# Moving the activation sums of a seven-product matrix scheme from VectorE to GpSimd, with later tile sums and reordered tile loads

## The chip, the cores and the metric

The kernel runs on one core of a Trainium2 chip. The metric is the device time of one execution in microseconds (us). Five engines work side by side: TensorE (PE in the rows; its weight loads are PEld), VectorE (DVE), ScalarE (ACT), GpSimd (POOL) and SyncE (SP, whose queue starts the weight DMAs). Each runs its own list of instructions in order; they meet at semaphores.

## The reference

Two transformer blocks over 256 tokens of width 2048 in float32. What the change touches is the feed-forward part of each block (called MLP here), once per block:

```
hf = rms_norm(x, g_ffn[layer])
x = x + (jax.nn.silu(hf @ w_gate[layer]) * (hf @ w_up[layer])) @ w_down[layer]
```

The hidden width is 5632, so each of the two MLPs streams about 138 MB of weights. The attention parts before and between them are computed by the same kernel and are not changed.

## The kernel before

Every float32 product is made of three passes of TensorE over rounded operands (fp32r): high weight with high activation, high weight with low activation, low weight with high activation. The weights come from memory as a stream of 512 KB units of 128x1024. For each unit ScalarE makes the high half (`split` in its list, L1140, `w_hi<-raw`), VectorE the low half (`split` in its list, L1649, `w_lo<-raw,w_hi`), and TensorE runs 12 matmuls (L622). All three buffers (`raw`, `w_hi`, `w_lo`) have four slots. So ScalarE may be four units ahead of TensorE at most; a unit's DMA starts when VectorE has read the unit four places before it; and the order of everything else is written out by hand as "after so many splits do this" (`steps(n, {k: [...]})`), a table for ScalarE and a like one for VectorE. An engine that waits inside such an entry also holds back its next splits.

An MLP has 3 groups of 3, 4 and 4 pairs of blocks (gate and up), each group followed by two pairs of "down" blocks. A block is 512 output columns for all 256 tokens. For 12 pairs in each MLP, `SEVEN`, the first two weight tiles of both blocks aren't multiplied in the plain way but by seven products of sums (a Strassen-like scheme). That needs:

- **tile sums** on GpSimd (`seven_sums(j)`, L554 to L557, four subtractions of 128x512 for each of two steps), over tiles that GpSimd loads itself (`load_seven(j)`, L538 two transfers of 768 KB, L540 one of 512 KB, into `heads` and, for odd j, `tab`). In the first line of `seven_sums` it waits for the third transfer. ScalarE (L1236, L1240) and VectorE (L1867) then round them (`preparing`, entries at three splits of the pair before).
- **activation sums** on VectorE (`sums_raw`, L1881 over 128x1024 into `tmp_c`, L1882 to L1885 over 128x256 each), then ScalarE's high half of them (`sums_hi`, L1246) and VectorE's low half (`sums_lo`, L1891). They are made three times in an MLP: once from the normed input (in the second pair of the first group, (0, up, 1), after split 7) and twice from the hidden values (in the pairs (0, up, 2) and (1, up, 2), after split 9). ScalarE's entry is at split 7 in the first case and 10 in the two others, VectorE's low half at 9 and at 11.
- **opening** (`open_seven`, L769): 24 matmuls of TensorE over the rounded sums; it waits for `act_ready` (from `sums_lo`) and `seven_ready`, and sits near the end of the pair before. For the first of an MLP it comes after the twelfth unit of (0, up, 1).
- **combining** (`combine`, L1898 to L1902 on VectorE, `first_out` and `third_in` on ScalarE, L1251 and L1256), then **closing** (`close_seven`, L769 again), for which TensorE waits for `combined` and `third_copied`. Where the pair being opened is (1, up, 3), `combine` is VectorE's entry at split 11 of (1, up, 2), right behind `sums_lo(True)`.

GpSimd's list in an MLP is a loop over j: wait until the tiles of j - 1 were used (`products_done`), `load_seven(j)`, `seven_sums(j)`. For the first j of an MLP the load waits for TensorE's second unit of the MLP, and the sums follow at once. During the first 16 units VectorE also transposes and norms the last parts of the activations (L1784, L1753), which TensorE needs from about the thirteenth unit on.

ScalarE's `gated` (L1294) is the gate function (silu) of a finished block, 128x512 twice; in (0, up, 1) it stands behind `sums_hi(False)` in the same entry.

Of the kernel before, what the change touches and what calls it, by code (L numbers as in the profile page):

```python
# [22 lines left out]
F32 = mybir.dt.float32  # L23
F32R = mybir.dt.float32r
I32 = mybir.dt.int32
ALU = mybir.AluOpType
# [8 lines left out]
CB = 4  # L35
NB = CB * P
# [160 lines left out]
def two_blocks(nc: bass.Bass, stream, seven_in, mem_in, mem_tok, x_in, x_tok, p_in, decay_in, vectors, rows_in,  # L197
               head_rows, consts, tables, positions, out):
    with ExitStack() as ctx:
# [3 lines left out]
        def sem(name):  # L203
            return ctx.enter_context(nc.semaphore(name))
# [101 lines left out]
        seven_hi_ready = sem("seven_hi_ready")  # L306
        seven_ready = sem("seven_ready")
        act_summed = sem("act_summed")
        act_hi_ready = sem("act_hi_ready")
        act_ready = sem("act_ready")  # L310
        products_done = sem("products_done")
# [84 lines left out]
        def raw7(step, i, n=1):  # L396
            return tiles(heads, step, i, n)
# [10 lines left out]
        def last_raw(j):  # L408
            return tab[:, 0:STEPS * NB].rearrange("p (s n) -> p s n", s=STEPS) if j % 2 else both_steps(heads, T4)
# [98 lines left out]
        def _(pool):  # L508
# [27 lines left out]
            def load_seven(j):  # L536
                for step in range(STEPS):
                    pool.dma_start(raw7(step, W11, 3), seven_in[j][:, step * 4 * NB:(step * 4 + 3) * NB])\  # L538
                        .then_inc(seven_landed[step], 16)
                pool.dma_start(last_raw(j), seven_in[j].rearrange("p (s n) -> p s n", s=STEPS)[:, :, 3 * NB:])\  # L540
                    .then_inc(last_landed, 16)

            def after_own(ins, n):

                ins.then_inc(pool_done, 1)
                pool.wait_ge(pool_done, n)

            def seven_sums(j):

                pool.wait_ge(last_landed, 16 * (j + 1))  # L550
                for step in range(STEPS):
                    own = 3 * (STEPS * j + step)
                    pool.wait_ge(seven_landed[step], 16 * (j + 1))
                    after_own(pool.tensor_tensor(raw7(step, T3), raw7(step, T2), raw7(step, T1), ALU.subtract), own + 1)  # L554
                    after_own(pool.tensor_tensor(raw7(step, T1), raw7(step, T1), raw7(step, W11), ALU.subtract), own + 2)
                    after_own(pool.tensor_tensor(raw7(step, T2), raw7(step, T2), raw7(step, T1), ALU.subtract), own + 3)
                    pool.tensor_tensor(last_raw(j)[:, step], last_raw(j)[:, step], raw7(step, T2), ALU.subtract)\  # L557
                        .then_inc(seven_summed, 1)

            for j in range(N_SEVEN):  # L560
                if j:
                    pool.wait_ge(products_done, j)
                else:
                    pool.wait_ge(w_used, U_MLP_AT[0] + 2)
                load_seven(j)
                seven_sums(j)

            pool.wait_ge(seven_used, N_SEVEN)
            pool.dma_start(tab[:, :], tables).then_inc(tab_landed, 16)
# [7 lines left out]
            for j in range(N_SEVEN, 2 * N_SEVEN):  # L577
                if j > N_SEVEN:
                    pool.wait_ge(products_done, j)
                else:  # L580
                    pool.wait_ge(w_used, U_MLP_AT[1] + 2)
                load_seven(j)
                seven_sums(j)
            pool.wait_ge(seven_used, 2 * N_SEVEN)
            pool.dma_start(tab[:, 0:2 * T], p_in).then_inc(p_landed, 16)
            load_row(B_ROW, ROWS.index("b_ple_gate_2"), bias_landed)
# [528 lines left out]
        def _(act):  # L1115
# [142 lines left out]
            def mlp(name, next_name, at, which, final=False, beside=None):  # L1258
# [43 lines left out]
                for g, n in enumerate(GROUPS):  # L1302
                    nd = n * CB // UK
                    for p in range(n):
                        pair = g, "up", p
                        j, after = (seventh(which, q) for q in all_pairs[all_pairs.index(pair):][:2])
                        early = {4: [lambda: hidden_hi(p - 1)]} if p else {}
                        if (g, p) == (0, 0):
                            during(2 * NU - 3, at)
                            wait_rows()  # L1310
                            gated()
                            split(3)
                            taken.add()
# [12 lines left out]
                        taken.add()  # L1326
# [300 lines left out]
        def _(dve):  # L1627
# [241 lines left out]
            def sums_raw(hidden, used):  # L1869

                if used:
                    dve.wait_ge(seven_used, used)
                dve.wait_ge(raw_read, units.value())
                if joined[0]:
                    dve.wait_ge(third_copied, joined[0])
                src_hi, src_lo = (mix_hi, mix_lo) if hidden else (norm_hi, norm_lo)
                by_sum = chunks(heads, sums_at(hidden) + CB).rearrange("p (s i n) -> p s i n", s=STEPS, i=4)
                s1, s2, s3, s4 = (by_sum[:, :, i] for i in range(4))
                by_part = tmp_c[:, :].rearrange("p (s i n) -> p s i n", s=STEPS, i=4)
                a11, a21, a12, a22 = (by_part[:, :, i] for i in range(4))  # L1880
# [24 lines left out]
            def mlp(name, next_name, at, which, final=False, beside=None, beside_last=None):  # L1905
# [52 lines left out]
                for g, n in enumerate(GROUPS):  # L1958
                    nd = n * CB // UK
                    for p in range(n):  # L1960
# [749 lines left out]
```

## Time and profile before

| | us |
|---|---|
| median of 3 runs | 2377.13 (2376.47 to 2378.82) |
| the profiled execution | 2374.19 |
| its span in the profile | 2372.0 |
| TensorE idle in the span | 18.5 |
| VectorE, ScalarE, GpSimd busy | 1949.5, 1223.2, 395.5 |

The profile is of one execution. What bounds the kernel is read first from the busy shares; as TensorE is nearly always busy, the few places where it is not are what a change off TensorE can win or lose. They are found with the waits of TensorE and with its busy time in stretches of 10 us; then the timeline around each shows who was late.

### The profile page before, as it was taken

Reading aid. Unit: us, or ns where it says so; the run is one execution under the profiler, and the core shown is the slowest. Engines: PE = TensorE matmul, PEld = TensorE weight load, DVE = VectorE, ACT = ScalarE, POOL = GpSimd, SP = SyncE. Lnnn points to the kernel's source line nnn. Section 1 sums busy time; section 2 is a strip of 40 time slices with the busy share of each in tenths; the row PEclk is TensorE's granted clock in tenths of the full one; section 3 lists DMA queues with packets and bytes.
Section 4 is the critical chain, followed back from the end, with each engine's and each line's share of the span. In section 5 each row is a group of like instructions: output and inputs, shape, how many; then the busy total and the mean of one; then the engine's idle time right before and its main releaser. Section 6 shows DMA issues by size and latency. Waiting matters only on the chain.

```text
span 2372.0 us, 30916 instructions
## 1 busy us (share of the span) xinstructions
PE 2353.5 (99%) x10692; PEld 1957.6 (83%) x10692; DVE 1949.5 (82%) x2542; ACT 1223.2 (52%) x1639; POOL 395.5 (17%) x290
## 2 busy tenths in 40 slices
PE   9999999999999999999999999999999999999999
PEld 8988888878888888888888888877878888888887
DVE  7788887879788977878897977987978898787885
ACT  6554555545455544545554445454545454464563
POOL 1000000211433434200000000021144343520000
PEclk9999999999999999999999999999999999999999
DMA  8755454665757676655555554565565666665655
GB/s 305 238 173 186 159 170 163 208 207 188 246 202 244 207 237 212 224 203 202 185 189 194 192 189 160 195 226 201 187 234 200 246 211 230 226 213 200 211 189 168
DMA packets 130337, 487.43 MB, mean 205 GB/s; under 512 B 14480, under 2 KB 15120, under 8 KB 129568
## 3 DMA queue, kind: packets, MB, share of 16 engines
q1 hardware_dynamic: 116736, 421.32, 53.0%
q0 software_dynamic: 13184, 64.02, 7.6%
q8 instruction: 86, 1.41, 0.2%
q14 instruction: 43, 0.35, 0.0%
q10 hardware_dynamic: 288, 0.33, 0.0%
HBM read 483.51 MB, written 2.10 MB: 205 GB/s over the span
## 4 chain that ended last, share of the span: by engine, by line
PE 93%; DVE 3%; DMA 1%; ACT 1%; POOL 1%; issue 1%; SPq 0%; ACTq 0%; DVEq 0%
PE acc L622 61%; PE pt L622 9%; PE po L622 9%; PE acc L769 4%; PE pt L769 3%; PE po L769 3%; DVE w_lo L1649 1%; DMA tab<-seven_in 1%; PE acc L985 1%; PE acc L627 1%; PE po L968 1%; PE acc L899 1%; DVE tmp_c L1784 1%; DVE norm_lo L1753 1%; PE po L960 1%
## 5 line engine op out<-in xcount | busy, mean ns | idle before, releaser
L1649 DVE TENSOR_TENSOR w_lo<-raw,w_hi 128x1024 fp32r<-128x1024 f32 x796 | 1022.0, 1299 | 314.2 <-ACT w_hi L1140 307.7
L1140 ACT ACTIVATE w_hi<-raw 128x1024 fp32r<-128x1024 f32 x795 | 831.8, 1058 | 784.1 <-PE acc L622 470.6
L622 PE MATMUL acc<-w_hi,norm_hi 128*128 128x512 f32 (+1 forms) x1460 | 568.6, 390 | 1.4 <-DVE norm_lo L1753 1.3
L622 PE MATMUL acc<-w_hi,norm_lo 128*128 128x512 f32 (+1 forms) x1460 | 565.3, 387 | 0.0
L622 PE MATMUL acc<-w_lo,norm_hi 128*128 128x512 f32 (+1 forms) x1460 | 387.8, 388 | 4.1 <-DVE w_lo L1649 4.0
L622 PE MATMUL acc<-w_hi,mix_hi 128*128 128x512 f32 x832 | 325.2, 391 | 0.3 <-ACT w_hi L1447 0.3
L622 PE MATMUL acc<-w_hi,mix_lo 128*128 128x512 f32 x832 | 324.1, 390 | 0.0
L622 PEld LDWEIGHTS acc<-w_lo,norm_hi 128*128 128x128 f32 x1460 | 272.7, 188 | 61.1 <-DVE w_lo L1649 5.4
L622 PEld LDWEIGHTS acc<-w_hi,norm_hi 128*128 128x128 f32 x1460 | 274.1, 188 | 57.6 <-issue 2.5
L622 PEld LDWEIGHTS acc<-w_hi,norm_lo 128*128 128x128 f32 x1460 | 274.1, 188 | 55.1
L622 PE MATMUL acc<-w_lo,mix_hi 128*128 128x512 f32 x832 | 222.5, 389 | 0.0
L622 PEld LDWEIGHTS acc<-w_hi,mix_hi 128*128 128x128 f32 x832 | 156.4, 188 | 33.3 <-ACT w_hi L1447 0.9
L622 PEld LDWEIGHTS acc<-w_lo,mix_hi 128*128 128x128 f32 x832 | 156.1, 188 | 32.8 <-DVE w_lo L1649 0.4
L622 PEld LDWEIGHTS acc<-w_hi,mix_lo 128*128 128x128 f32 x832 | 156.5, 188 | 32.2
L538 POOL DMA_DIRECT2D heads<-seven_in x48 | 26.3, 550 | 913.6 <-PE acc L622 415.2
L1784 DVE STREAM_TRANSPOSE tmp_c<-tmp_b 32x256 f32<-32x256 f32 x352 | 153.5, 436 | 5.0
L1867 DVE TENSOR_TENSOR heads_r<-heads,heads_r 128x2048 fp32r<-128x2048 f32 (+1 forms) x60 | 131.9, 2198 | 0.9 <-ACT heads_r L1236 0.9
L554 POOL TENSOR_TENSOR heads<-heads 128x512 f32<-128x512 f32 x48 | 80.4, 1676 | 218.2 <-DMA heads<-seven_in 109.1
L1236 ACT ACTIVATE heads_r<-heads 128x2048 fp32r<-128x2048 f32 x48 | 91.6, 1908 | 43.4 <-POOL tab L557 24.3
L622 PE MATMUL po<-w_hi,norm_hi 128*128 128x512 f32 x240 | 93.4, 389 | 0.0
L622 PE MATMUL po<-w_hi,norm_lo 128*128 128x512 f32 x240 | 93.4, 389 | 0.0
L622 PE MATMUL pt<-w_hi,norm_hi 128*128 128x512 f32 x240 | 93.4, 389 | 0.0
(354 smaller groups left out, 2938.8 us busy)
## 6 DMA issues: line engine op xcount, KB each, us to landing
raw<-stream SPq DMA_DIRECT2D x795, 512.0 KB, 3.7
heads<-seven_in POOLq DMA_DIRECT2D x48, 768.0 KB, 7.1
heads<-seven_in POOLq DMA_DIRECT2D x12, 512.0 KB, 10.4
tab<-seven_in POOLq DMA_DIRECT2D x12, 512.0 KB, 9.6
heads<-x_in POOLq DMA_DIRECT2D x4, 512.0 KB, 8.0
x<-x_tok POOLq DMA_DIRECT2D x4, 512.0 KB, 7.0
x<-mem_tok POOLq DMA_DIRECT2D x2, 1024.0 KB, 8.2
x<-x_tok POOLq DMA_DIRECT2D x1, 2048.0 KB, 9.9
```

The source lines that it names most:

```text
L538: pool.dma_start(raw7(step, W11, 3), seven_in[j][:, step * 4 * NB:(step * 4 + 3) * NB])\
L554: after_own(pool.tensor_tensor(raw7(step, T3), raw7(step, T2), raw7(step, T1), ALU.subtract), own + 1)
L622: last = pe.matmul(out_[:, c * NB:c * NB + width], a[:, k * T + c * P:k * T + (c + 1) * P], w[:, s, kk * width:(kk + 1) * width], start=cl ...
L627: last = pe.matmul(out_[:, c * T:(c + 1) * T], w[:, s, kk * NB + c * P:kk * NB + (c + 1) * P], a[:, k * T:(k + 1) * T], start=clear and i ...
L769: last = pe.matmul(bank, a, w, start=clear and i == 0, stop=i == 2, skip_group_check=True)
L899: last = pe.matmul(dst[:, at:at + width], src[:, q * T + t * P:q * T + (t + 1) * P], heads[:, k * T:k * T + width], start=t == 0 and i == ...
L960: last = pe.matmul(po[:, n % 2, t * width:(t + 1) * width], prob_t[:, kk * T + t * P:kk * T + (t + 1) * P], heads[:, v:v + width], start=t ...
L1140: act.activation(w_hi[:, (units.fixed - 1) % RING, :], src, ACT.Copy).then_inc(w_hi_ready, 1)
L1236: act.activation(hi7(part, W11, 4), raw7(part, W11, 4), ACT.Copy).then_inc(seven_hi_ready, 1)
L1649: dve.tensor_tensor(w_lo[:, s, :], src, w_hi[:, s, :].bitcast(F32), ALU.subtract)\
L1784: last = dve.transpose(to_rows[:, :, :, of * 32:(of + 1) * 32], rows[of * 32:(of + 1) * 32, :, :, to * 32:(to + 1) * 32])
L1867: dve.tensor_tensor(dst, src, hi.bitcast(F32), ALU.subtract).then_inc(seven_ready, 1)
```

## The change

- GpSimd makes the activation sums. VectorE, where it made them, only raises a new semaphore `sums_due`; GpSimd waits for it in `act_sums(j)`, which stands in its list behind `seven_sums(j)` for the j of (0, up, 2), (0, down, 1) and (1, up, 3). The same five operations follow, the first three each with a wait for its own result.
- In (0, up, 1) ScalarE's entry at split 7 keeps only `gated`; `sums_hi(False)` moves to split 9. VectorE's `sums_lo(False)` moves from split 9 to 10 and the last part of `preparing` from 10 to 11. The entries in (0, up, 2) and (1, up, 2) stay.
- The first tile sums of each MLP wait for TensorE's twelfth unit; their loads start as before.
- Of the three tile loads the 512 KB one goes second instead of third, and the wait for it stands before the fourth subtraction instead of the first.

```
@@ load_seven, seven_sums, act_sums (GpSimd)
                     pool.dma_start(raw7(step, W11, 3), seven_in[j][:, step * 4 * NB:(step * 4 + 3) * NB])\
                         .then_inc(seven_landed[step], 16)
-                pool.dma_start(last_raw(j), seven_in[j].rearrange("p (s n) -> p s n", s=STEPS)[:, :, 3 * NB:])\
-                    .then_inc(last_landed, 16)
+                    if step == 0:
+                        pool.dma_start(last_raw(j), seven_in[j].rearrange("p (s n) -> p s n", s=STEPS)[:, :, 3 * NB:])\
+                            .then_inc(last_landed, 16)
...
-                pool.wait_ge(last_landed, 16 * (j + 1))
                 for step in range(STEPS):
...
+                    pool.wait_ge(last_landed, 16 * (j + 1))
                     pool.tensor_tensor(last_raw(j)[:, step], last_raw(j)[:, step], raw7(step, T2), ALU.subtract)\
                         .then_inc(seven_summed, 1)
+
+            def act_sums(j):
+
+                hidden = SEVEN[j % N_SEVEN] != (0, "up", 2)
+                pool.wait_ge(sums_due, acts_summed.add())
...
+                after_own(pool.tensor_tensor(tmp_c[:, :], chunks(src_hi, 0).bitcast(F32), chunks(src_lo, 0).bitcast(F32),
+                                             ALU.add))
+                after_own(pool.tensor_tensor(s1, a21, a22, ALU.add))
+                after_own(pool.tensor_tensor(s2, s1, a11, ALU.subtract))
+                pool.tensor_tensor(s3, a11, a21, ALU.subtract)
+                pool.tensor_tensor(s4, a12, s2, ALU.subtract).then_inc(act_summed, 1)
...
                 load_seven(j)
+                if j == 0:
+                    pool.wait_ge(w_used, U_MLP_AT[0] + 12)
                 seven_sums(j)
+                if sums_behind(j):
+                    act_sums(j)
@@ mlp (ScalarE)
-                            sums = {7: [lambda: sums_hi(False), gated]}
+                            sums = {7: [gated], 9: [lambda: sums_hi(False)]}
@@ sums_raw (VectorE)
-                link(dve.tensor_tensor(tmp_c[:, :], chunks(src_hi, 0).bitcast(F32), chunks(src_lo, 0).bitcast(F32), ALU.add))
-                link(dve.tensor_tensor(s1, a21, a22, ALU.add))
-                link(dve.tensor_tensor(s2, s1, a11, ALU.subtract))
-                dve.tensor_tensor(s3, a11, a21, ALU.subtract)
-                dve.tensor_tensor(s4, a12, s2, ALU.subtract).then_inc(act_summed, 1)
+                dve.sem_inc(sums_due, 1)
@@ mlp (VectorE)
-                                    9: [lambda: sums_lo(False)], 2 * NU - 1: [take_up]}
-                            steps(2 * NU, both(early, preparing(after, 6, 8, 10), joining(after, 13), sums))
+                                    10: [lambda: sums_lo(False)], 2 * NU - 1: [take_up]}
+                            steps(2 * NU, both(early, preparing(after, 6, 8, 11), joining(after, 13), sums))
```

## Rows read from the trace of the kernel before

**Rows 1.** The page, its first part: busy time of each engine.

```profile
PE 2353.5 (99%) x10692; PEld 1957.6 (83%) x10692; DVE 1949.5 (82%) x2542; ACT 1223.2 (52%) x1639; POOL 395.5 (17%) x290
```

**Rows 2.** Waits of TensorE, whole span: total us, times, longest.

```profile
PE pt L769 <- issue: 4.5, 2, 2.3
PE acc L622 <- DVE w_lo L1649: 4.0, 2, 2.6
PE acc L769 <- DVE heads_r L1867: 1.9, 1, 1.9
PE acc L622 <- DVE norm_lo L1753: 1.3, 1, 1.3
```

**Rows 3.** Timeline of VectorE, last norm parts: start, us, operation, count.

```profile
447.22 1.67 DVE L1753 SCALAR_TENSOR_TENSOR norm_lo<-tmp_c,vec,norm_hi 128x256 fp32r<-128x256 f32 x4
...
461.78 3.75 DVE L1753 SCALAR_TENSOR_TENSOR norm_lo<-tmp_b,vec,norm_hi 128x256 fp32r<-128x256 f32 x4
...
1580.28 5.83 DVE L1753 SCALAR_TENSOR_TENSOR norm_lo<-tmp_c,vec,norm_hi 128x256 fp32r<-128x256 f32 x4
```

**Rows 4.** One tile load (us to landing, issued 1759.5), then the timeline behind it.

```profile
heads<-seven_in POOLq DMA_DIRECT2D x1, 768.0 KB, 8.0
...
1773.37 2.35 POOL L554 TENSOR_TENSOR heads<-heads 128x512 f32<-128x512 f32 x1 [12.03 <-DMA tab<-seven_in]
...
1781.57 1.92 ACT L1236 ACTIVATE heads_r<-heads 128x2048 fp32r<-128x2048 f32 x1 [5.48 <-POOL tab L557]
...
1791.12 1.20 PE L622 MATMUL acc<-w_lo,norm_hi 128*128 128x512 f32 x4 [1.32 <-DVE w_lo L1649]
```

**Rows 5.** Timeline of (0, up, 1) in the first MLP; last row: chain of waits.

```profile
499.74 1.22 DVE L1881 TENSOR_TENSOR tmp_c<-norm_hi,norm_lo 128x1024 f32<-128x1024 f32 x1
...
502.71 1.06 ACT L1246 ACTIVATE heads_r<-heads 128x1024 fp32r<-128x1024 f32 x1 [4.85 <-DVE heads L1885]
503.67 1.25 ACT L1294 ACTIVATE tmp_d<-acc,r_tok 128x512 f32<-128x512 f32 x2
...
510.38 1.22 DVE L1891 TENSOR_TENSOR heads_r<-heads,heads_r 128x1024 fp32r<-128x1024 f32 x1
...
511.70 0.47 PE L769 MATMUL pt<-heads_r,norm_hi 128*128 128x512 f32 x1 [2.24 <-issue]
...
519.00 10.88 PE acc L622 x48
```

**Rows 6.** Stretches: us, then busy PE PEld DVE ACT POOL, granted clock, DMA share, GB/s.

```profile
510.00:520.00 10.00, 8.30 (x30) 6.72 (x31) 6.14 (x6) 1.06 (x1) 0.70 (x2) 0.83 0.67 211
...
1585.00:1595.00 10.00, 7.36 (x33) 5.77 (x32) 7.94 (x6) 1.92 (x3) 2.15 (x2) 1.00 0.50 168
...
1635.00:1645.00 10.00, 7.70 (x27) 5.94 (x26) 7.55 (x7) 2.12 (x3) 0.00 (x0) 0.83 0.66 218
```

**Rows 7.** Single lines: duration in ns, min/median/max, first and last start.

```profile
L555 POOL TENSOR_TENSOR heads<-heads x48: 1288/1751/3218, 451.5 to 2115.1; 128x512 f32<-128x512 f32 x48
...
L1649 DVE TENSOR_TENSOR w_lo<-raw,w_hi x796: 1209/1225/2329, 7.7 to 2358.2; 128x1024 fp32r<-128x1024 f32 x199
...
L1867 DVE TENSOR_TENSOR heads_r<-heads,heads_r x60: 1210/2282/3384, 496.3 to 2128.1; 128x2048 fp32r<-128x2048 f32 x48, 128x1024 fp32r<-128x1024 f32 x12
```

**Rows 8.** Timeline of (1, up, 2) in the first MLP, up to the closing.

```profile
754.51 1.06 ACT L1246 ACTIVATE heads_r<-heads 128x1024 fp32r<-128x1024 f32 x1 [5.22 <-DVE heads L1885]
...
757.70 1.22 DVE L1891 TENSOR_TENSOR heads_r<-heads,heads_r 128x1024 fp32r<-128x1024 f32 x1
...
760.75 0.69 DVE L1902 TENSOR_TENSOR po<-tmp_c,po 128x512 f32<-128x512 f32 x1
...
762.78 0.39 PE L769 MATMUL pt<-heads_r,norm_hi 128*128 128x512 f32 x1
```

**Rows 9.** Timeline of (0, up, 2) in the first MLP.

```profile
564.05 1.07 ACT L1246 ACTIVATE heads_r<-heads 128x1024 fp32r<-128x1024 f32 x1 [5.26 <-DVE heads L1885]
...
568.25 1.07 PE L622 MATMUL acc<-w_lo,mix_hi 128*128 128x512 f32 x4
```

More of the change, by code:

```diff
@@ L308, in two_blocks @@
         act_summed = sem("act_summed")
+        sums_due = sem("sums_due")
         act_hi_ready = sem("act_hi_ready")
@@ L539, in load_seven @@
                         .then_inc(seven_landed[step], 16)
-                pool.dma_start(last_raw(j), seven_in[j].rearrange("p (s n) -> p s n", s=STEPS)[:, :, 3 * NB:])\
-                    .then_inc(last_landed, 16)
-            def after_own(ins, n):
+                    if step == 0:
+                        pool.dma_start(last_raw(j), seven_in[j].rearrange("p (s n) -> p s n", s=STEPS)[:, :, 3 * NB:])\
+                            .then_inc(last_landed, 16)
+            own = Tally()
+            acts_summed = Tally()
@@ L545, in after_own @@
+            def after_own(ins):
                 ins.then_inc(pool_done, 1)
-                pool.wait_ge(pool_done, n)
+                pool.wait_ge(pool_done, own.add())
             def seven_sums(j):
-                pool.wait_ge(last_landed, 16 * (j + 1))
                 for step in range(STEPS):
-                    own = 3 * (STEPS * j + step)
                     pool.wait_ge(seven_landed[step], 16 * (j + 1))
-                    after_own(pool.tensor_tensor(raw7(step, T3), raw7(step, T2), raw7(step, T1), ALU.subtract), own + 1)
-                    after_own(pool.tensor_tensor(raw7(step, T1), raw7(step, T1), raw7(step, W11), ALU.subtract), own + 2)
-                    after_own(pool.tensor_tensor(raw7(step, T2), raw7(step, T2), raw7(step, T1), ALU.subtract), own + 3)
+                    after_own(pool.tensor_tensor(raw7(step, T3), raw7(step, T2), raw7(step, T1), ALU.subtract))
+                    after_own(pool.tensor_tensor(raw7(step, T1), raw7(step, T1), raw7(step, W11), ALU.subtract))
+                    after_own(pool.tensor_tensor(raw7(step, T2), raw7(step, T2), raw7(step, T1), ALU.subtract))
+                    pool.wait_ge(last_landed, 16 * (j + 1))
@@ L557, in seven_sums @@
                     pool.tensor_tensor(last_raw(j)[:, step], last_raw(j)[:, step], raw7(step, T2), ALU.subtract)\
                         .then_inc(seven_summed, 1)
+            def act_sums(j):
+                hidden = SEVEN[j % N_SEVEN] != (0, "up", 2)
+                pool.wait_ge(sums_due, acts_summed.add())
+                src_hi, src_lo = (mix_hi, mix_lo) if hidden else (norm_hi, norm_lo)
+                by_sum = chunks(heads, sums_at(hidden) + CB).rearrange("p (s i n) -> p s i n", s=STEPS, i=4)
+                s1, s2, s3, s4 = (by_sum[:, :, i] for i in range(4))
+                by_part = tmp_c[:, :].rearrange("p (s i n) -> p s i n", s=STEPS, i=4)
+                a11, a21, a12, a22 = (by_part[:, :, i] for i in range(4))
+                after_own(pool.tensor_tensor(tmp_c[:, :], chunks(src_hi, 0).bitcast(F32), chunks(src_lo, 0).bitcast(F32),
[4 more added lines that the diff above has]
+                pool.tensor_tensor(s4, a12, s2, ALU.subtract).then_inc(act_summed, 1)
@@ L560, in _, with sums_behind @@
+            def sums_behind(j):
+                g, kind, p = SEVEN[j % N_SEVEN]
+                return (g, kind, p) in ((0, "up", 2), (0, "down", 1), (1, "up", 3))
             for j in range(N_SEVEN):
@@ L582, in _ @@
                 load_seven(j)
+                if j == N_SEVEN:
+                    pool.wait_ge(w_used, U_MLP_AT[1] + 12)
                 seven_sums(j)
+                if sums_behind(j):
+                    act_sums(j)
             pool.wait_ge(seven_used, 2 * N_SEVEN)
@@ L1875, in sums_raw @@
                     dve.wait_ge(third_copied, joined[0])
[L1876 to L1880, printed above, removed]
-                link(dve.tensor_tensor(tmp_c[:, :], chunks(src_hi, 0).bitcast(F32), chunks(src_lo, 0).bitcast(F32), ALU.add))
-                link(dve.tensor_tensor(s1, a21, a22, ALU.add))
-                link(dve.tensor_tensor(s2, s1, a11, ALU.subtract))
-                dve.tensor_tensor(s3, a11, a21, ALU.subtract)
-                dve.tensor_tensor(s4, a12, s2, ALU.subtract).then_inc(act_summed, 1)
+                dve.sem_inc(sums_due, 1)
             def sums_lo(hidden):
```

## Prediction, written before the changed kernel was run

> **What bounds the kernel now.** I read the busy shares first: TensorE is busy for 2353.5 of 2372.0 us [rows 1]. The other engines matter only where TensorE stands still, 18.5 us in all. TensorE's waits [rows 2] name 11.7 us of this, and each lies in a place that the change touches. The "issue" wait is twice the opening of an MLP's first seven-product pair; the timeline shows who was really late: VectorE's low half of the activation sums (L1891) ends at 510.38 + 1.22 = 511.60, and TensorE starts at 511.70 after 2.24 us of idleness [rows 5]; the second MLP has the same stall at 2.3. The 1.3 and the 2.6 are norm parts and weight halves of VectorE that ran late while GpSimd made the first tile sums. The 1.9 and 1.32 come behind tile sums that started late [rows 4]. Besides, the granted clock is 0.83 over 10 us around both openings and 1.00 elsewhere, around the 2.6 us stall too [rows 6]. A mean of 0.83 over 10 us is 3.4 us at 1.2 instead of 2.4 GHz and costs 1.7 us each time, 3.4 for the two.
>
> A weight unit takes TensorE 10.88 / 4 = 2.72 us [rows 5]. In what follows "late" means later than TensorE's need by this rhythm.
>
> **First tile sums later.** An L1753 group of four takes 1.67 us alone, but 3.75 and 5.83 with GpSimd beside it [rows 3]: 2.1 and 4.2 us. TensorE waited behind these 1.3 and 2.6 us [rows 2]. The sums now start after the twelfth unit, when these groups are done, so both stalls go: -3.9. Their own user, ScalarE's first rounding, comes some nine units (24 us) after that, and eight subtractions take 8 x 1.29 = 10.3 alone and about 18 if each is held, so they hide. They now collide with the weight halves of units 13 to 19; each may take 2.33 instead of 1.23 [rows 7], still under 2.72. I take nothing for that; bound 0 to 1 us in each MLP.
>
> **Tile loads in another order.** The first 768 KB land 8.0 us after 1759.5, at 1767.5, but the first subtraction starts at 1773.37, when the third transfer is there [rows 4]. Now it can start 5.8 us earlier; the second step's tiles land last, about where the third transfer did, by when the first step is summed. ScalarE waited 5.48 us for the sums here [rows 4], and TensorE 1.32 and, one pair earlier, 1.9 behind it. Both go: -3.2 (4.0 - 2.6 = 1.4 by the rounded waits, 1.32 by the row), bound 0 to -3.2. Elsewhere the earlier sums meet slack.
>
> **What the sums cost on GpSimd.** The trace shows it only at 512 columns: 1.29 us undisturbed [rows 7]. From both sides: 1024 columns between 1.29 and 2.58, 256 between 0.65 and 1.29, the five together between 3.9 and 7.7. To choose, I use the holding: L1649 grows from 1.23 to 2.33 and L1867 from 2.28 to 3.38, both by 1.10 at most [rows 7]. That is what a 512-column subtraction blocks VectorE, leaving 0.19 of its 1.29 as fixed part. So 0.19 + 2.20 = 2.39, four times 0.19 + 0.55 = 0.74, sum 5.35; with the waits between them 5.7 (estimate). VectorE took 502.71 - 499.74 = 2.97 for the same [rows 5]. The holding goes both ways: the longest L555 is 1.93 over the shortest, one L1867 of 2.28 in its way; so a w_lo of 1.23 costs it about 0.87.
>
> The page "GPSIMD Engine Reference" of the Trainium skill (section "Engine selection") speaks against this change: it puts two-input elementwise work on VectorE, GpSimd being about twice as slow. By its ratio 2.97 us would be about 5.9, against my 5.7; no run here has shown these widths on GpSimd.
>
> **The opening of (0, up, 1), twice.** The sums are due at 499.74. ScalarE no longer waits there: its gate (1.25) starts when TensorE ends the block, at 511.70 - 2.24 - 4 x 2.72 = 498.6, then come a high half (to 500.9), the last tile rounding and another high half (to about 503); only then, at split 9, does it wait for the sums. GpSimd's first operation starts before VectorE has a new weight half to make; its second then meets one w_lo (0.87), the third the 2.28 us L1867 of split 8 (1.93), the fourth the next w_lo (0.87); the fifth is free. End: 499.74 + 5.7 + 3.7 = 509.1. Queued behind ScalarE's wait is the high half of split 10, and behind that on VectorE the low half of split 10 and then, as the diff moves it, the low half of the sums: 1.06 (L1246) + 1.06 + 1.22 + 1.22 = 4.5, so ready at 513.6 against 511.60 now. The stall grows from 2.2 to about 4.2: +2.0, twice +4.0. The clock falls again, as before: 0. Bounds: with nothing held the sums end at 505.4, ready at 509.9, stall 0.5 (that is a rival below); with 7.7 instead of 5.35 the stall is 6.5, +4.3 each.
>
> **The sums in (0, up, 2), twice.** Due 2.97 before 564.05, at 561.08 [rows 9]. VectorE has one w_lo at hand, which goes first (1.1); then it waits for ScalarE and holds nothing. End 561.1 + 1.1 + 5.7 = 567.9, 3.8 later than now, and ScalarE waits for it as it does now. Its next high half then ends near 569.9; TensorE wants it when the unit before ends, 568.25 + 1.07 = 569.3 [rows 9]. Stall 0.6, twice +1.2; bound 0 to 1.5 each.
>
> **The sums in (1, up, 2), twice.** The same 3.8 us later start of L1246. TensorE has more weight units in hand here, since an opening of 24 matmuls lies between, but VectorE's `combine` is queued behind L1891 (now at 757.70 [rows 8]) at split 11, and the closing waits for it. Now it ends at 760.75 + 0.69 = 761.44 and TensorE closes at 762.78 [rows 8], a margin of 1.3. So a stall of 3.8 - 1.3 = 2.5, less some slack of starting: 2.4, twice +4.8. Bounds: 0 if the five end within 4.4 us of being due, 4.5 with 7.7. GpSimd's next tile load (it stands behind `act_sums`) leaves 3 us later; the new order gives 5.8 back, so 0.
>
> **Sum.** -3.9 - 3.2 + 4.0 + 1.2 + 4.8 = +2.9; I carry +2.8. VectorE loses 6 x 2.97 = 17.8 us of work, but no end hangs on its total. Against the profiled execution (2374.19, its span 2372.0 and 2.2 around it) that is 2377.0; the median of the runs lies 2.9 above that execution, so 2377.13 + 2.8 = 2379.9.
>
> **Rivals.** (a) The sums come in time, faster. If VectorE's operations don't get in between GpSimd's five, or are done earlier, the opening's stall is 0.5 instead of 2.2 and 2.3: -3.5, and the clock stays up: -3.4. With the rest: -3.9 - 3.2 - 6.9 + 6.0 = -8.0, 2369.1. It decides from sums that end before 511.6 - 4.5 = 507.1, 7.4 us after they are due. For it: the median L555 is 1.75, not 3.22 [rows 7], so many aren't held long; against it: L1867, the longest holder, stands exactly there.
>
> (b) The new stalls at the closings of (1, up, 2) cost the clock as well, slower. The mechanism is `combine` behind the later L1891; the price is 2.4 of stall and 1.7 of clock each; it decides once a stall there is as long as the 2.24 that dropped the clock at the opening. Against it: 2.64 us near 1586 did not [rows 6]. +2.8 + 3.4 = +6.2, 2383.3. The page "TensorE: Matmul & The Clock Gate" of the Trainium skill (section "HAM oscillation — how this bites in real kernels") says that gaps in the matmul stream can bring the low clock back; the rows show that a gap of this length sometimes does.
>
> (c) The edits on the tile sums don't do what they should: the collision merely moves to units 13 to 19, where TensorE waits as long as now. +3.9, so +6.7, 2383.8. Against it: VectorE has no norm parts there, and a weight half held for its full 2.33 us [rows 7] still fits into the 2.72 of a unit.
>
> **How the numbers follow.** Forecast 0.45 (own range 2377 to 2382.5; 0.38 of it within 0.2%, 0.07 slower), (a) 0.27, (b) 0.20, (c) 0.08. Of no change a measurement here can tell about 0.2%, 4.8 us. Faster 0.27, same 0.38, slower 0.35. The range, 2368 to 2385.5, takes in (a), (b) and (c) and most of the bounds.
>
> **What would show it.** GpSimd rows of `tmp_c<-norm_hi,norm_lo` near 2.4 us and of 128x256 near 0.75 undisturbed; the opening's "issue" stall at 4 us (forecast) or under 1 (a), with a clock of 0.83 or 1.00; a new wait of TensorE for VectorE's L1902 of about 2.4 us in (1, up, 2); no waits for L1753; GpSimd's first subtraction of a pair some 5 us earlier behind its load. The prediction is wrong if GpSimd's 256-column operations cost much more or less than 0.74, or if VectorE's operations hold it less than they hold the tile sums.

## The result, and the profile after

The changed kernel takes 2391.42 us (2388.72 to 2395.2, 4 runs) against 2376.8 (2375.54 to 2378.82, 4 runs) of the kernel before: ratio 1.0062, interval 1.0044 to 1.0079. It is slower by 14.6 us. The prediction was 2379.9 with a range up to 2385.5, so it was wrong in size, and "within 0.2%" was the wrong case.

The profiled execution took 2395.2 us, 21.0 more than that of before (2374.19). The page's first part, to be held against [rows 1]:

```profile
PE 2360.0 (99%) x10692; PEld 1961.8 (82%) x10692; DVE 1941.6 (81%) x2512; ACT 1223.3 (51%) x1639; POOL 437.4 (18%) x320
```

Same matmuls, 6.5 us more busy time: that is low clock, as the stretches below show. VectorE, which lost six times 2.97 = 17.8 us of work, is busy only 7.9 us less: its other operations got longer. TensorE stands still for 2393.4 - 2360.0 = 33.4 us instead of 18.5. Its waits (total us, times, longest), to be held against [rows 2]:

```profile
PE pt L801 <- issue: 11.6, 2, 6.2
PE acc L654 <- issue: 5.2, 2, 2.7
PE pt L801 <- DVE po L1925: 4.8, 4, 1.8
PE pt L654 <- DVE w_lo L1681: 3.7, 2, 1.9
PE acc L654 <- DVE mix_lo L2171: 1.8, 1, 1.8
```

The four entries of [rows 2] are changed altogether: the norm part, the late rounding `heads_r` and both old weight-half stalls are gone. The opening's wait (L769 before, L801 now) has grown from 4.5 to 11.6; three kinds are new. L654 behind "issue" is (0, up, 2), L801 behind L1925 is mostly the closing in (1, up, 2), and the w_lo pair comes 17 us behind those closings. The last line lies at the kernel's start, away from the change.

The first opening on the timeline (start, us, operation, count, idle before it and who ended it), against [rows 5]; GpSimd, then ScalarE, then TensorE:

```profile
502.19 2.41 POOL L573 TENSOR_TENSOR tmp_c<-norm_hi,norm_lo 128x1024 f32<-128x1024 f32 x1 [20.10 <-DVEq L1908]
504.68 1.60 POOL L575 TENSOR_TENSOR heads<-tmp_c 128x256 f32<-128x256 f32 x1
506.35 2.67 POOL L576 TENSOR_TENSOR heads<-heads,tmp_c 128x256 f32<-128x256 f32 x1
509.10 1.58 POOL L577 TENSOR_TENSOR heads<-tmp_c 128x256 f32<-128x256 f32 x1
510.65 0.72 POOL L578 TENSOR_TENSOR heads<-tmp_c,heads 128x256 f32<-128x256 f32 x1
...
511.40 1.06 ACT L1278 ACTIVATE heads_r<-heads 128x1024 fp32r<-128x1024 f32 x1 [7.20 <-POOL heads L578]
...
515.89 0.76 PE L801 MATMUL pt<-heads_r,norm_hi 128*128 128x512 f32 x1 [6.20 <-issue]
```

The 128x256 operation takes 0.72 alone, 1.60 with one weight half of VectorE in its way and 2.67 with the 2.28 us rounding. ScalarE waits 7.20 us for the end of it. In (0, up, 2) only the second of the five is held, by one weight half, and yet TensorE waits there too. GpSimd, ScalarE and TensorE in (0, up, 2), then TensorE at the closing of (1, up, 2) and behind it:

```profile
565.27 2.39 POOL L573 TENSOR_TENSOR tmp_c<-mix_hi,mix_lo 128x1024 f32<-128x1024 f32 x1 [22.32 <-DVEq L1908]
567.74 1.60 POOL L575 TENSOR_TENSOR heads<-tmp_c 128x256 f32<-128x256 f32 x1
569.42 0.74 POOL L576 TENSOR_TENSOR heads<-heads,tmp_c 128x256 f32<-128x256 f32 x1
...
571.70 1.06 ACT L1278 ACTIVATE heads_r<-heads 128x1024 fp32r<-128x1024 f32 x1 [8.76 <-POOL heads L578]
572.66 2.94 ACT L1172 ACTIVATE w_hi<-raw 128x1024 fp32r<-128x1024 f32 x3
...
573.79 0.47 PE L654 MATMUL acc<-w_hi,mix_hi 128*128 128x512 f32 x1 [2.51 <-issue]
...
774.31 0.47 PE L801 MATMUL pt<-heads_r,norm_hi 128*128 128x512 f32 x1 [1.75 <-DVE po L1925]
...
793.31 1.97 PE L654 MATMUL pt<-w_lo,norm_hi 128*128 128x512 f32 x4 [1.87 <-DVE w_lo L1681]
```

The granted clock (after the POOL column) around them, against [rows 6]:

```profile
510.00:520.00 10.00, 4.11 (x10) 3.27 (x11) 5.87 (x6) 3.89 (x4) 1.37 (x2) 0.68 0.46 157
570.00:580.00 10.00, 7.49 (x26) 5.74 (x25) 6.24 (x7) 5.91 (x6) 1.58 (x3) 0.83 0.44 150
770.00:780.00 10.00, 8.25 (x37) 6.52 (x36) 9.93 (x11) 5.18 (x6) 7.78 (x5) 1.00 0.82 304
790.00:800.00 10.00, 8.13 (x29) 6.23 (x28) 8.44 (x10) 7.97 (x7) 0.00 (x0) 0.83 0.59 189
1650.00:1660.00 10.00, 6.54 (x22) 5.27 (x22) 5.77 (x5) 2.86 (x4) 0.00 (x0) 0.66 0.51 172
1710.00:1720.00 10.00, 8.82 (x32) 7.18 (x33) 8.81 (x11) 6.04 (x7) 0.00 (x0) 0.83 0.54 162
```

Two low stretches before, five now, and the two old ones are deeper. The stretch of the closing, 770 to 780, kept 1.00.

### The profile page after: what moved, and what is told of

Read it like the earlier page. It is cut to its first block and busy times, and to the rows that moved or that the text cites. A ratio compares the mean times of both kernels' runs of the same rounds, so it can differ in the third digit from the quotient of the medians.

```text
span 2393.4 us, 30947 instructions
## 1 busy us (share of the span) xinstructions
PE 2360.0 (99%) x10692; PEld 1961.8 (82%) x10692; DVE 1941.6 (81%) x2512; ACT 1223.3 (51%) x1639; POOL 437.4 (18%) x320
## 5 line engine op out<-in xcount | busy, mean ns | idle before, releaser
L1681 DVE TENSOR_TENSOR w_lo<-raw,w_hi 128x1024 fp32r<-128x1024 f32 x796 | 1041.2, 1322 | 330.6 <-ACT w_hi L1172 323.0
L654 PE MATMUL acc<-w_hi,norm_hi 128*128 128x512 f32 (+1 forms) x1460 | 568.5, 390 | 0.1
L654 PE MATMUL acc<-w_hi,norm_lo 128*128 128x512 f32 (+1 forms) x1460 | 565.3, 387 | 0.0
L654 PE MATMUL acc<-w_lo,norm_hi 128*128 128x512 f32 (+1 forms) x1460 | 387.4, 387 | 0.0
L654 PE MATMUL acc<-w_hi,mix_hi 128*128 128x512 f32 x832 | 326.5, 392 | 7.0 <-issue 5.2
L654 PE MATMUL acc<-w_hi,mix_lo 128*128 128x512 f32 x832 | 325.5, 391 | 0.0
L654 PEld LDWEIGHTS acc<-w_hi,norm_hi 128*128 128x128 f32 x1460 | 274.2, 188 | 55.9 <-issue 0.8
L654 PEld LDWEIGHTS acc<-w_hi,norm_lo 128*128 128x128 f32 x1460 | 274.1, 188 | 55.0
L654 PEld LDWEIGHTS acc<-w_lo,norm_hi 128*128 128x128 f32 x1460 | 273.0, 188 | 55.8
L654 PE MATMUL acc<-w_lo,mix_hi 128*128 128x512 f32 x832 | 224.4, 392 | 0.0
L654 PEld LDWEIGHTS acc<-w_hi,mix_hi 128*128 128x128 f32 x832 | 157.1, 189 | 40.7 <-issue 6.0
L654 PEld LDWEIGHTS acc<-w_lo,mix_hi 128*128 128x128 f32 x832 | 157.7, 190 | 33.1
L654 PEld LDWEIGHTS acc<-w_hi,mix_lo 128*128 128x128 f32 x832 | 157.2, 189 | 32.6
L654 PE MATMUL pt<-w_hi,norm_hi 128*128 128x512 f32 x240 | 93.9, 391 | 0.0
L654 PE MATMUL pt<-w_hi,norm_lo 128*128 128x512 f32 x240 | 93.9, 391 | 0.0
L654 PE MATMUL po<-w_hi,norm_hi 128*128 128x512 f32 x240 | 93.4, 389 | 0.0
L654 PE MATMUL po<-w_hi,norm_lo 128*128 128x512 f32 x240 | 93.4, 389 | 0.0
```

The source lines that it names most:

```text
L654: last = pe.matmul(out_[:, c * NB:c * NB + width], a[:, k * T + c * P:k * T + (c + 1) * P], w[:, s, kk * width:(kk + 1) * width], start=cl ...
L1681: dve.tensor_tensor(w_lo[:, s, :], src, w_hi[:, s, :].bitcast(F32), ALU.subtract)\
```

## The experiments

### The edits taken apart

**a1_late_tiles**: before, with the later first tile sums alone.

```diff
                 load_seven(j)
+                if j == 0:
+                    pool.wait_ge(w_used, U_MLP_AT[0] + 12)
                 seven_sums(j)
```

(The second MLP has the same wait against its own start.)

> The kernel before with only the first tile sums of each MLP behind TensorE's twelfth unit. Theory L (lateness): the stalls of 1.3 and 2.6 us near 465 and 1588 go (-3.9), but GpSimd now holds VectorE's weight halves right ahead of (0, up, 1); VectorE comes some 2.2 us later to the activation sums, so the opening's stall grows from 2.2 to about 4.4 in both MLPs (+4.4): within 1 us of before, about 2377.3. Rival (the move is free, as predicted): openings at 2.2 and 2.3 still, about 2372.9.

Measured: 2372.61 us, ratio 0.9983 (0.9972 to 0.9995). TensorE's stalls behind the norm parts are gone (1.27 and 2.64), but the first MLP has new ones:

```profile
PE pt L773 <- issue: 5.5, 2, 2.8
...
PE acc L626 <- ACT w_hi L1144: 1.3, 1, 1.3
```

So part of the gain is given back in the openings (5.5 instead of 4.5) and just ahead of the first (1.3, ScalarE's high half, late because ScalarE had waited for VectorE's sums). A late tile rounding (1.70) and a weight half (1.07) are new in the first MLP, and the 1.9 of the second has shrunk to 0.46. The time is the rival's 2372.9; the stalls lie between the two expectations.

**a2_order**: before, with the reordered loads alone.

```diff
                         .then_inc(seven_landed[step], 16)
-                pool.dma_start(last_raw(j), ...).then_inc(last_landed, 16)
+                    if step == 0:
+                        pool.dma_start(last_raw(j), ...).then_inc(last_landed, 16)
...
-                pool.wait_ge(last_landed, 16 * (j + 1))
                 for step in range(STEPS):
...
+                    pool.wait_ge(last_landed, 16 * (j + 1))
                     pool.tensor_tensor(last_raw(j)[:, step], last_raw(j)[:, step], raw7(step, T2), ALU.subtract)
```

> The kernel before with only the 512 KB tile load second and its wait before the fourth subtraction. Prediction's step: the stalls of 1.95 and 1.32 us near 1756 and 1791 go, -3.3, about 2373.5. Rival: the tile sums that start 3 to 6 us earlier collide with VectorE's busy entries elsewhere (new wait of TensorE for w_lo, as near 793 and 1930 in the changed kernel, 1.9 each): about 2377.

Measured: 2369.13 us, ratio 0.9962 (0.9948 to 0.9977), some 7 us, twice the expected. The stalls of 1.9 and 1.32 went as expected, the one of 2.64 in the second MLP too, which the order was not expected to touch; new ones came in return (0.88, 0.81, 0.75 and 0.53), and the profiled execution is only 3.2 us shorter than that of before. The rest of the 7 us is not seen in a trace. TensorE's longest waits are now

```profile
PE pt L770 <- issue: 4.5, 2, 2.3
PE acc L623 <- DVE norm_lo L1754: 1.3, 1, 1.3
PE acc L623 <- DVE w_lo L1650: 1.1, 2, 0.9
```

**a4_tiles_both**: both of these together, nothing else.

> Both edits on the tile sums, activation sums still on VectorE. Theory L: -3.9 - 3.3 + 4.4 = -2.8, about 2374. Rival (both free): -7.2, about 2369.6. The activation sums' own cost is then the changed kernel's 2391.4 less this.

Measured: 2369.66 us, ratio 0.9967 (0.9956 to 0.9978), so -6.6 us by the medians. The sum of the tile steps in the prediction (-7.1) fits, though the parts do not add up to it: the late sums alone gave -3.6 by the medians, and order alone already -7.1. In the profiled execution the four stalls are gone, but others have come, so that TensorE stands still 15.0 us instead of 18.5: 2.76 us at each opening instead of 2.24 and 2.30, 1.29 ahead of the first, and in the second MLP

```profile
1904.84 1.21 PE L627 MATMUL pt<-w_lo,norm_hi 128*128 128x512 f32 x4 [1.56 <-DVE w_lo L1654]
```

**a3_sums_only**: the changed kernel with both tile edits undone, so that only the activation sums are on GpSimd.

> Activation sums on GpSimd with the entries as in the change, tile sums as before. If nearly all of the loss is theirs: opening stalls of about 4 us (not 6.2 and 5.4, since VectorE isn't late here), 2.6 in both (0, up, 2), 1.75 in both (1, up, 2), clock falling at four to six places: +3.8 + 5.2 + 3.5 + 3.4 to 6.8 of clock = +16 to +19, 2393 to 2396. Rival (much of the loss comes from the tile edits working together with it): under +8, below 2385.

Measured: 2395.4 us, ratio 1.0072 (1.0055 to 1.0089), some 17 us slower than before. TensorE's waits:

```profile
PE pt L796 <- issue: 8.2, 2, 4.1
PE acc L649 <- issue: 6.2, 2, 3.1
PE pt L796 <- DVE po L1920: 3.9, 2, 2.1
```

The openings' stalls are 4.12 and 4.09: the prediction's 4.2 to a tenth. The closings give 3.9 of the prediction's 4.8. What is not in its sum is the middle line, (0, up, 2), 6.2 instead of 1.2; and the clock, 0.83 from 510 to 520 and from 1710 to 1720 and

```profile
570.00:580.00 10.00, 8.26 (x30) 6.75 (x31) 8.27 (x10) 6.54 (x7) 0.00 (x0) 0.83 0.47 151
1600.00:1610.00 10.00, 8.51 (x30) 6.87 (x31) 8.38 (x6) 2.12 (x2) 2.50 (x2) 0.83 0.65 207
1650.00:1660.00 10.00, 5.91 (x16) 4.36 (x15) 5.76 (x5) 3.90 (x4) 0.11 (x1) 0.67 0.55 184
```

TensorE's busy time here is 2359.9, 6.4 over that of before.

### Was the slack in (0, up, 2) mis-read?

**s1_slack**: before, with VectorE making its first hidden sum three times (two useless repeats), so that the sums end later by a known time, with no GpSimd in it.

```diff
+                for _ in range(3 if hidden else 1):
-                link(dve.tensor_tensor(tmp_c[:, :], chunks(src_hi, 0).bitcast(F32), ...))
+                    link(dve.tensor_tensor(tmp_c[:, :], chunks(src_hi, 0).bitcast(F32), ...))
```

> The kernel before with the first operation of the hidden activation sums (128x1024 on VectorE) made three times: ScalarE gets these sums 2.4 us later in both (0, up, 2) and (1, up, 2), with no GpSimd in it. The prediction's slack of 3.2 us for the next high half in (0, up, 2): no stall there. Theory S (the high half is wanted one weight unit of 2.72 us earlier, slack 0.5): a stall of about 1.9 us in each (0, up, 2). Both: about 1.1 us at the closings after (1, up, 2), margin 1.3. Time under the prediction's slack about +2, under S about +6, each with 1.7 more for every stall that drops the clock.

Measured: 2390.55 us, ratio 1.0045 (1.0026 to 1.0065). In (0, up, 2) TensorE stands still for

```profile
571.99 1.20 PE L622 MATMUL po<-w_lo,norm_hi 128*128 128x512 f32 x4 [1.97 <-DVE w_lo L1649]
```

and for 2.13 in the second MLP. A delay of 2.5 us gives stalls of about 2.0, without any sum on GpSimd. But TensorE waits here for VectorE's weight half, which stands in VectorE's list right behind the lengthened sums (at 563.94 before, at 570.72 here), not for ScalarE's high half, of which the prediction had taken the slack. So this run shows that the place has 0.4 to 0.5 us to spare, and not by itself whose. ScalarE's slack is in the trace of the kernel before, ScalarE's high halves behind `sums_hi` and the first matmul that needs one:

```profile
565.02 2.94 ACT L1140 ACTIVATE w_hi<-raw 128x1024 fp32r<-128x1024 f32 x3
...
566.44 0.39 PE L622 MATMUL acc<-w_hi,mix_hi 128*128 128x512 f32 x1
```

The first of the three ends near 566.0, 0.4 us ahead of its use. It is the same first matmul into `acc` that waits at 573.79 in the changed kernel.

The rest of the 14 us lies in the closings (1.18 and 0.81), in two late weight halves (0.8 and 0.7), in tile roundings (1.5 more than before), in 1.8 us at the start of the kernel and in 5.3 us of low clock, at other places than these two stalls.

### Was it the place of the sums?

**b1_due_early**: the changed kernel, the sums due behind VectorE's split 6 instead of 7 and 9.

```diff
-                            sums = {7: [lambda: sums_raw(False, which * N_SEVEN), gated],
+                            sums = {6: [lambda: sums_raw(False, which * N_SEVEN)], 7: [gated],
...
-                                sums = {9: [lambda: sums_raw(True, used)], 11: [lambda: sums_lo(True)]}
+                                sums = {6: [lambda: sums_raw(True, used)], 11: [lambda: sums_lo(True)]}
```

> The changed kernel with the activation sums due behind split 6 in place of 7 (normed) and 9 (hidden); ScalarE's and VectorE's entries stay. If the loss is the sums' length on GpSimd behind a due time that was set for VectorE: the stalls of (0, up, 2) and at the closings of (1, up, 2) go (-5.2, -3.5) and the clock with them (-3.4 to -5), the openings shrink by 3.4 us each: about 2372. Rival (GpSimd's work costs by holding VectorE's port wherever it is): the stalls move to other waits for w_lo and the time stays over 2385.

Measured: 2383.27 us, ratio 1.0026 (1.0015 to 1.0037), between the two expectations. The long stalls of (0, up, 2) and the closings of (1, up, 2) are gone, weight-half stalls of 1.4 stand in (0, up, 2). But the openings hardly shrank (6.00 and 4.57 us). GpSimd was due 5.9 us earlier there and ended only 3 us earlier:

```profile
496.25 4.33 POOL L573 TENSOR_TENSOR tmp_c<-norm_hi,norm_lo 128x1024 f32<-128x1024 f32 x1 [16.76 <-DVEq L1908]
500.66 1.60 POOL L575 TENSOR_TENSOR heads<-tmp_c 128x256 f32<-128x256 f32 x1
502.34 1.60 POOL L576 TENSOR_TENSOR heads<-heads,tmp_c 128x256 f32<-128x256 f32 x1
504.01 2.67 POOL L577 TENSOR_TENSOR heads<-tmp_c 128x256 f32<-128x256 f32 x1
506.64 1.70 POOL L578 TENSOR_TENSOR heads<-tmp_c,heads 128x256 f32<-128x256 f32 x1
```

VectorE's rounding (2.28) had started 0.2 us before the first one, and its later work met the four others, so all five were held.

**b3_due_hidden**: only the second of these two edits.

> As b1, for the hidden sums alone: stalls in (0, up, 2) and (1, up, 2) and their clock go, the openings stay at 6 and 5 us: about 2379. Rival: over 2387.

Measured: 2385.14 us, ratio 1.0035 (1.0023 to 1.0046), between the two expectations; openings 6.41 and 5.38, the rest as in b1_due_early. So the hidden sums' place is worth some 6 of the 14.6 us, and the openings are their own matter.

**c1_unheld**: the changed kernel, VectorE's rounding that stood in GpSimd's way moved behind it.

```diff
-                            steps(2 * NU, both(early, preparing(after, 6, 8, 11), joining(after, 13), sums))
+                            steps(2 * NU, both(early, preparing(after, 6, 10, 11), joining(after, 13), sums))
```

> The changed kernel, but in (0, up, 1) VectorE's rounding of the second step's tiles (2.28 us, L1899) moves from its split 8 to its split 10, so that it doesn't stand in GpSimd's way while the five sums are made; everything else stays. Theory H (GpSimd's operations are held by VectorE's two-input ones): the third sum starts 1.9 us earlier, the five end 7.4 us after they are due instead of 9.3, and ScalarE's L1278 starts 1.9 earlier. But the moved rounding then lies between that and VectorE's low half of the sums, so the opening's stall stays near 6 us (5.0 to 6.5) and the time within 3 us of 2391.4. Rival: GpSimd's sums are slow by themselves: their end stays 9.3 us after due.

Measured: 2392.1 us, ratio 1.0067 (1.0052 to 1.0083), openings 6.48 and 5.23.

```profile
499.76 2.40 POOL L573 TENSOR_TENSOR tmp_c<-norm_hi,norm_lo 128x1024 f32<-128x1024 f32 x1 [20.09 <-DVEq L1908]
...
507.06 1.06 ACT L1278 ACTIVATE heads_r<-heads 128x1024 fp32r<-128x1024 f32 x1 [5.29 <-POOL heads L578]
```

From the first operation to ScalarE's use: 7.3 us, against 511.40 - 502.19 = 9.2 in the changed kernel. The 1.9 us of holding are real; and the stall stays, since the rounding now lies ahead of the low half. Whichever comes first, the other pays.

**v3_gpsimd_early**: as b1_due_early (the hidden sums too), but the sums due ahead of the rounding in split 6, and `sums_lo(False)` at split 9.

```diff
-                            sums = {7: [lambda: sums_raw(False, which * N_SEVEN), gated],
-                                    10: [lambda: sums_lo(False)], 2 * NU - 1: [take_up]}
-                            steps(2 * NU, both(early, preparing(after, 6, 8, 11), joining(after, 13), sums))
+                            sums = {6: [lambda: sums_raw(False, which * N_SEVEN)], 7: [gated],
+                                    9: [lambda: sums_lo(False)], 2 * NU - 1: [take_up]}
+                            steps(2 * NU, both(early, sums, preparing(after, 6, 8, 11), joining(after, 13)))
...
```

> GpSimd makes the activation sums, as in the changed kernel, but they are due behind VectorE's split 6, in (0, up, 1) ahead of the tile rounding of that entry, and there VectorE's low half goes from split 10 to 9. Theory (the change's idea fits, only its place is late): due about 496.6, then 5.7 us alone and 1.93 + 2 x 0.87 held = 505.9; ScalarE's L1278 to 507.0, VectorE's L1914 to 508.5 to 509.5, where TensorE wants it at 509.0: opening stalls of 0 to 0.8 instead of 6.2 and 5.4, (0, up, 2) keeps about 1.4 + 0.3 as in b1_due_early, no closing stall, no low clock at the openings: 2391.4 less 25 us = 2366 to 2372. Rival (the holding grows with whatever stands there, as in b1_due_early, where the five took 12 us): stalls of 3 us or more stay at the openings with the low clock, 2375 to 2383.

Measured: 2377.72 us, ratio 1.0004 (0.9993 to 1.0014), between the two expectations; openings 3.07 and 1.62. Both engines pay while they meet:

```profile
496.37 2.41 POOL L573 TENSOR_TENSOR tmp_c<-norm_hi,norm_lo 128x1024 f32<-128x1024 f32 x1 [16.76 <-DVEq L1908]
496.38 4.55 DVE L1899 TENSOR_TENSOR heads_r<-heads,heads_r 128x2048 fp32r<-128x2048 f32 x1
```

VectorE's rounding takes 4.55 instead of 2.28, and the five end 11.2 us after they started, 1.9 more than expected: a second rounding fell among them.

### The same freedom without GpSimd

**v1_vector_early**: a4_tiles_both, with VectorE making the sums itself, behind split 6.

> Both edits on the tile sums, activation sums on VectorE but behind split 6. If the due time is what counts and not the engine, the openings' stalls of 2.8 us (and 1.3 before the first) shrink or go, with their clock: 2360 to 2366. Rival (VectorE is too full behind split 6, its weight halves come late): 2369 or more.

Measured: 2369.8 us, ratio 0.9973 (0.9961 to 0.9984), no gain over a4_tiles_both, as the rival had it. The sums were early, but the first opening's stall stayed at 2.76 (the second's shrank to 1.86): ScalarE's entry still made its sums and its gate ahead of the next high half.

**v2_early_ready**: v1, with the consumers moved too.

```diff
 ScalarE
-                            sums = {7: [lambda: sums_hi(False), gated]}
+                            sums = {7: [gated], 8: [lambda: sums_hi(False)]}
 VectorE
-                                    9: [lambda: sums_lo(False)], 2 * NU - 1: [take_up]}
-                            steps(2 * NU, both(early, preparing(after, 6, 8, 10), joining(after, 13), sums))
+                                    8: [lambda: sums_lo(False)], 2 * NU - 1: [take_up]}
+                            steps(2 * NU, both(early, sums, preparing(after, 6, 8, 10), joining(after, 13)))
```

> The kernel before with both tile edits, VectorE making the activation sums itself but behind split 6 (as in the run before), and besides: in (0, up, 1) ScalarE's gate stays at split 7 and its high half of the sums goes to split 8, VectorE's low half of the sums to split 8, both sums ahead of the tile roundings. ScalarE then never waits for the sums ahead of a weight half (3.6 us now), and the low half ends near 507 instead of 511.7, where TensorE wants it at 509.0. Expected: the opening stalls of 2.76 and 1.86 us go, and with them the low clock at 510 (1.7 us): 2369.8 - 6.3 = 2363.5, 2361 to 2367. Rival: another chain is right behind (the 2.28 us rounding L1872 or the weight halves), and the stall only shrinks: 2367 to 2370.

Measured: 2363.2 us (2362.39 to 2365.63, 5 runs), ratio 0.9942 (0.9928 to 0.9955): faster than both kernels, and 0.3 us from the expectation. No opening stall, granted clock 1.00 around both openings, and TensorE's waits and busy time are

```profile
PE 2350.3 (100%) x10692; PEld 1954.4 (83%) x10692; DVE 1940.0 (82%) x2542; ACT 1225.2 (52%) x1639; POOL 394.5 (17%) x290
...
PE po L627 <- DVE w_lo L1654: 2.4, 4, 1.1
PE pt L774 <- DVE po L1907: 1.2, 2, 0.6
```

## Why the prediction was wrong, point by point

TensorE's idle time and busy time in the profiled executions, prediction against measurement:

| step of the prediction | predicted us | measured us |
|---|---|---|
| four old tile stalls (1.3, 2.6, 1.9, 1.32) | -7.1 | -7.2 |
| openings (4.5 before) | +4.0 | +7.0 |
| (0, up, 2), twice | +1.2 | +5.2 |
| closings of (1, up, 2), twice | +4.8 | +3.5 |
| weight halves 17 us behind them | 0 | +3.7 |
| other closings (0.8 and 0.54) | 0 | +1.3 |
| start of the kernel (1.75, 0.3 before) | 0 | +1.4 |
| low clock (busy time) | 0 | +6.5 |
| sum | +2.9 | +21.4 |

The spans of the two executions differ by 21.4 (2393.4 - 2372.0). The row on the start has nothing to do with the change, and the profiled execution lies 3.8 us over the median of its kernel, so the medians' 14.6 is the fairer size of it.

**Right: what the sums cost on GpSimd.** 2.39 was said for 1024 columns, 0.74 for 256 (2.38 to 2.41 and 0.71 to 0.74 measured), +0.87 for a weight half in the way (1.60) and +1.93 for a rounding (2.67). From the first operation to ScalarE it was 9.2 at the opening (9.4 said) and 571.70 - 565.27 = 6.4 in (0, up, 2) (6.8 said). On VectorE the same widths take 1.22 and 0.42; a ratio of 1.7 to 2.0. The page "GPSIMD Engine Reference" of the Trainium skill (section "Engine selection") says about twice as slow, and this trace agrees.

**Right in the number, not in the mechanism: the tile edits' sum**, by a4_tiles_both -6.6 against -7.1. The order alone gave 7 instead of 3.2, and in the profiled execution of a4_tiles_both 3.8 of the 7.2 us of old stalls came back as new ones. That execution is 4.8 us shorter than that of before; that the medians are 6.6 apart, so near the forecast, is luck as far as the traces show.

**Failed: "both stalls go: -3.9"**, with "I take nothing for that; bound 0 to 1 us in each MLP" for the collision with units 13 to 19. The weight halves there did fit into 2.72, as said, so TensorE did not wait for them. But at the opening TensorE waits for VectorE's chain, and what TensorE no longer lost at the norm parts it lost there, since VectorE came no sooner. TensorE ahead of and behind the norm parts and VectorE's `take_up` in (0, up, 1), on the timeline of before and then of the changed kernel:

```profile
463.33 1.07 PE L622 MATMUL acc<-w_lo,norm_hi 128*128 128x512 f32 x4
467.59 1.07 PE L622 MATMUL acc<-w_lo,norm_hi 128*128 128x512 f32 x4
477.31 1.40 DVE L1704 SCALAR_TENSOR_TENSOR tmp_b<-acc,r_tok,tmp_d 128x512 f32<-128x512 f32 x2
```

```profile
465.11 1.07 PE L654 MATMUL acc<-w_lo,norm_hi 128*128 128x512 f32 x4
467.83 1.07 PE L654 MATMUL acc<-w_lo,norm_hi 128*128 128x512 f32 x4
479.49 1.40 DVE L1736 SCALAR_TENSOR_TENSOR tmp_b<-acc,r_tok,tmp_d 128x512 f32<-128x512 f32 x2
```

At 465 both engines of the changed kernel are 1.8 us behind those of before, for reasons that lie ahead of the change. Then TensorE, without its stall, is only 0.2 behind and stays so up to the opening (it is ready for it at 509.69 against 509.46). VectorE is 2.2 behind at `take_up`, and the first sum follows at 502.19 instead of 499.74 [rows 5]: the collision took from it all that the shorter norm parts had given and 0.4 to 0.7 us more. So by TensorE's time the sums are due 2.2 us later, 1.5 of it because TensorE comes sooner; in the second MLP 1.3. a1_late_tiles shows the same without sums on GpSimd: in its first MLP the stalls at and just ahead of the opening are 4.1 us, where the norm parts and the opening together had cost 3.5; in the second 2.75 against 4.9. By TensorE's waits that makes -1.6 of the -3.9 (its time, 3.6 us less by the medians, can't tell the two apart: its interval is from 1.2 to 6.7 us). In a3_sums_only, with the tile sums at their old place, the openings' stalls are 4.12 and 4.09, as predicted, but TensorE still waits 1.7 and 2.8 us at the old places; in the changed kernel they are 6.20 and 5.38, 3.4 more.

**Failed: the slack in (0, up, 2), "TensorE wants it when the unit before ends, 568.25 + 1.07 = 569.3".** That puts the want 8.2 us after the sums are due. The high half behind `sums_hi` belongs to the unit before in TensorE's list, which in the kernel before starts at 566.44, 5.4 us after 561.08; in a3_sums_only the want is 5.4 us after due as well, in the changed kernel 573.79 - 2.51 - 565.27 = 6.0. With one unit (2.72) less, the slack is 0.4 to 0.5 us instead of 3.2, and the predicted lateness of 3.8 us would have given a stall of 3.4: a3_sums_only has 3.15 and 3.10, the changed kernel 2.51 and 2.74. s1_slack supports the small slack of the place, by another engine's wait. The term is +5.2 instead of +1.2.

**Failed: "The clock falls again, as before: 0".** It fell longer at the openings (0.68 and 0.66 in the two stretches, 0.83 before) and at three further places: the new stalls of 2.51 and 2.74 in (0, up, 2) and the one of 1.87 at 793. Rival (b) had the mechanism, but at the closings; there 1.75 us left the clock at 1.00. The busy time grew by 6.5, in a3_sums_only by 6.4. The page "TensorE: Matmul & The Clock Gate" of the Trainium skill (section "HAM oscillation — how this bites in real kernels") has gaps in the matmul stream bring back the low clock; the row of 570 to 580 agrees (0.83 with a stall of 2.51 us), that of the closing, 770 to 780, does not (1.00 with one of 1.75).

**Roughly right: the closings**, 1.75 and 1.76 instead of 2.4.

**Failed: "the new order gives 5.8 back, so 0"**, for what comes behind the closings. There the next pair's tile sums hold two pairs of VectorE's weight halves (3.79 and 4.38 us instead of 2.36), then come the transposes, and TensorE waits 1.87 and 1.86 us for the next half. Neither the late load nor the late closing explains it alone. a4_tiles_both, which has neither, has the stall of 1.56 at 1904.84 in the same place of its second MLP; b1_due_early, b3_due_hidden and v3_gpsimd_early, without the stall at the closing, keep it (1.8 to 1.9); a3_sums_only, which has both but not the tile edits, has only 0.74 in the first MLP and none in the second. So the earlier tile sums of the new order have a part in it, and how it divides stays open.

**Rival (a)**, sums in time, was given 0.27. The experiments that tried to bring it about (b1_due_early, v3_gpsimd_early) ended at 1.0026 and 1.0004: even when due earlier, the sums meet VectorE's two-input work. The same freedom used on VectorE (v2_early_ready) gave 0.9942.

## What to carry to other kernels

Taking 18 us of work off an engine that isn't the bound is worth nothing where the work sits on a chain with 0 to 2 us of slack: its latency counts, and it grew from 2.97 to between 6.4 and 9.2 us. Nor is the engine freed by as much: against a4_tiles_both (1943.6) VectorE of the changed kernel (1941.6) is busy only 2.0 us less. Before pricing a delay on such a chain, name the instruction queued behind the wait and the very unit that TensorE needs it for; one unit wrong was 4 us here. And a stall taken away ahead of another wait is gained only as far as the engine waited for there comes sooner as well; otherwise it comes back at the next wait, as 1.3 us of it did in the first MLP.

## What the runs showed of the hardware

- GpSimd's two-input operations and VectorE's take turns, operation by operation: the one that started first keeps its length, and the other is stretched by most of the time that they would have shared. The first sum of 2.40 us grew to 4.33 when a 2.28 us rounding had started 0.2 us before it (b1_due_early), and the rounding grew to 4.55 when the sum had started 0.01 us before it (v3_gpsimd_early). A weight half of 1.22 us in the way cost a sum of 256 columns 0.87 us, a rounding of 2.28 us cost it 1.93.
- A single stall of 2.51 us (in (0, up, 2)) came with a granted clock of 0.83 in its stretch of 10 us; one of 2.64 us [rows 6] and those of 1.97 in s1_slack and 1.75 at the closing did not. Of the two alike at 793 (1.87) and 1930 (1.86) only the first did. What tells them apart stays open: the length alone doesn't.
- The opening's clock went from 0.83 to 0.68 when its stall grew from 2.24 to 6.20 us, and to 1.00 in v2_early_ready, where the stall is gone.
